# Hybrid decoder trunk on one core: half of the sample pages issued by GpSimd

## The chip, the cores and the metric

The kernel runs on one core of one Trainium2 chip. The metric is the device time of one execution in microseconds (us); lower is better. Three runs of the kernel before stand beside one profiled execution, from which the trace comes. All data are float32.

## The reference, cut to what matters

The program is one inference step of two layers for a prompt group of 512 tokens and a sample group of 8 sequences with 4 new tokens each. Layer 0 mixes tokens with native sparse attention, layer 1 with a gated delta rule; each is followed by a feed-forward block. The change touches only the sample part of layer 0. Each sample sequence has a past of 2048 tokens, held in 16 pages of 128 tokens that lie anywhere in a shared cache; a page table says where.

```
kc = compress_blocks(kv_full[:, :, 0], pe_k, w1_k, w2_k)      # pages, columns 0 and 1
vc = compress_blocks(kv_full[:, :, 1], pe_v, w1_v, w2_v)
p_cmp = masked_softmax(s, cvis) ...                           # attention over the compressed blocks
imp = jnp.einsum('bkgtn,nj->bktj', p_cmp, cmp_to_slc(nc, ns)) # importance of each 64-token block
top_s, top_i = lax.top_k(imp, ...)                            # 16 blocks are chosen
o_slc = attention over the chosen blocks of kv_full[:, :, 2:4] # pages, columns 2 and 3
o_win = attention over the last 512 tokens
o = g0 * o_cmp + g1 * o_slc + g2 * o_win
```

So of every page two halves are read: one "to compress" (128 KB) and one "to attend to" (128 KB).

## The kernel before

The program is written by hand: each engine has its own instruction stream, and semaphores tie the streams together. Names are `sp` (SyncE, issues nearly all loads), `pool` (GpSimd, issues the stores and adds a few squares), `pe` (TensorE), `act` (ScalarE) and `dve` (VectorE).

The sample part of layer 0 is a loop over the 8 sequences s = 0 to 7 on `pe`. In the pass of sequence s the stream of `pe` holds, in this order: `new_rows(s)`, `scores(s)` (L942 to L946), the first quarter of `compress(s + 1)` (L902, 16 matmuls in the trace), `importance(s)` (L950), the second quarter, `turn_window(s)` (L958), the third, `window_values(s)` (L967), the fourth, `values(s)` (L974 to L986) and `compressed(s + 1)` (L911, L914). So the next sequence is compressed inside the pass of the present one, and everything on `pe` that stands behind a quarter waits if that quarter waits. The last matmul of `compress(s)` adds one to the semaphore `w1_used`; the compression of the prompt has added one before, so `w1_used` is s + 1 once `compress(s)` is done. The last matmul of `values(s)` adds one to `so_done`.

Four buffers take pages: `page_cmp[0]`, `page_cmp[1]` for the halves to compress and `page_kv[0]`, `page_kv[1]` for the halves to attend to; sequence s uses the one of its parity. `wcache[s % 2]` takes the window rows of the cache, which `pool` then stores to the output `win_o` (L582), after which `win_stored` tells `sp` that the buffer is free.

Before it can issue a page, the issuing engine loads its number from the table in SBUF into a register. `places(s)` (L487) does this 16 times: a TENSOR_LOAD and two register instructions each. `pages(...)` (L492) issues the 16 loads of one buffer, with two register instructions ahead of each. In the kernel before both are done by `sp`, in `sequence(s)`: the 16 numbers, a wait, 16 pages to compress, a wait, 16 pages to attend to, and the window. The pages to compress of sequence s >= 3 wait for `w1_used` >= s - 1, that is for the end of `compress(s - 2)`, which used the same buffer.

Of the kernel before, what the change touches and what calls it, by code (L numbers as in the profile page):

```python
# [23 lines left out]
P = 128  # L24
D = 1024
KT = D // P
TP, NS, DT = 512, 8, 4
# [5 lines left out]
NPAGE, PAGE = 16, 128  # L33
PAST = NPAGE * PAGE
NPHYS = (NS * NPAGE * 5 + 3) // 4
# [87 lines left out]
def build(nc, x_in, mem_in, w_in, common_in, prompt_in, sample_in, gdn_in, pages_in, win_in, mcache_in, conv_in,  # L123
          state_in, table_in, y_out, kv_out, win_out, conv_out_p, conv_out_s, state_out_p, state_out_s, mem_out):
    with ExitStack() as ctx:
        sem = lambda name: ctx.enter_context(nc.semaphore(name))
# [27 lines left out]
        a = rest()  # L154
# [12 lines left out]
        a = free()  # L167
# [152 lines left out]
        in_prompt_t, in_sample_t, in_gdn_t = sem("in_prompt_t"), sem("in_sample_t"), sem("in_gdn_t")  # L320
        in_panel = [sem(f"in_panel{s}") for s in range(4)]
        in_cmp = [sem(f"in_cmp{s}") for s in range(2)]
        in_pages = [sem(f"in_pages{s}") for s in range(2)]
        in_mcache, in_mkv1, in_conv = sem("in_mcache"), sem("in_mkv1"), sem("in_conv")
        in_state = [sem(f"in_state{h}") for h in range(GH)]
# [132 lines left out]
        block = ctx.enter_context(nc.Block())  # L458


        @block.sync
        def _(sp):
            sp.dma_start(common_ap, common_in).then_inc(in_common, 16)
            sp.dma_start(memT, mem_in).then_inc(in_mem, 16)

            def panel(i):
                slot = i % 4
                if i >= 4:
                    f = free_at[i - 4]
                    if f == "w1":  # L470
                        sp.wait_ge(w1_used, NS)
                    elif f == "window":
                        sp.wait_ge(so_done, NS)
                        for b in range(2):
                            sp.wait_ge(win_stored[b], 16 * (NS // 2))
                    else:
                        sp.wait_ge(*f)
                sp.dma_start(ring[slot], w_in[src[i]]).then_inc(in_panel[slot], 16)

            panel(0)  # L480
            sp.dma_start(xT, x_in).then_inc(in_x, 16)
            for i in range(1, 4):
                panel(i)
            sp.dma_start(pages_sb[:, :], table_in).then_inc(in_table, 16)

            def places(s):
                return [sp.value_load(pages_sb[0:1, s * NPAGE + p:s * NPAGE + p + 1], min_val=0, max_val=NPHYS - 1)  # L487
                        for p in range(NPAGE)]

            def pages(s, at, to, cols, landed):  # L490
                for p in range(NPAGE):
                    sp.dma_start(to[s % 2][:, p, :],  # L492
                                 pages_in[bass.ds(at[p], 1), :, cols].rearrange("a p n -> (a p) n"))\
                        .then_inc(landed[s % 2], 16)

            def sequence(s):

                at = places(s)
                if s >= 3:
                    sp.wait_ge(w1_used, s - 1)  # L500
                pages(s, at, page_cmp, slice(0, 2 * P), in_cmp)
                if s == 1:
                    sp.wait_ge(prompt_done, 24)
                if s >= 2:
                    sp.wait_ge(so_done, s - 1)
                pages(s, at, page_kv, slice(2 * P, 4 * P), in_pages)
                if s >= 2:
                    sp.wait_ge(win_stored[s % 2], 16 * (s // 2))
                window(s)

            def window(s):
                sp.dma_start(wcache[s % 2], win_in[s]).then_inc(in_pages[s % 2], 16)

            for i in range(4, 14):
                panel(i)
                if i == 8:
                    sp.wait_ge(memn_ready, 2 * KT)
                    sp.wait_ge(mem_stored, 32)
                    sp.dma_start(mcache[0], mcache_in[0].rearrange("s p n -> p s n")).then_inc(in_mcache, 16)
                if i == 10:  # L520
                    sp.wait_ge(in_table, 16)
                    pages(0, places(0), page_cmp, slice(0, 2 * P), in_cmp)
            sp.wait_ge(prod_done, 7 * NSA_U)
            window(0)
            pages(0, places(0), page_kv, slice(2 * P, 4 * P), in_pages)
            sp.wait_ge(mix_mem, 5)
            sp.dma_start(prompt_ap, prompt_in).then_inc(in_prompt_t, 16)
            sp.wait_ge(w1_used, 1)
            sp.wait_ge(psum_ready, 2)
            sp.dma_start(sample_ap, sample_in).then_inc(in_sample_t, 16)  # L530
            for s in range(1, NS):
                sequence(s)
            for i in range(15, wbase["gdn_in"] + 14):
                if i == 15:
                    sp.wait_ge(smax_ready, NS)
                panel(i)
                if i == wbase["gdn_in"] + 3:
                    sp.wait_ge(prod_done, 7 * ubase["gdn_in"])
                    sp.wait_ge(*read_out(ubase["gdn_in"] - 1, "c21"))
                    sp.wait_ge(sq_used, KT + 2)  # L540
                    sp.dma_start(mkv[1], mem_out[1]).then_inc(in_mkv1, 16)
                    sp.dma_start(gdn_ap, gdn_in).then_inc(in_gdn_t, 16)
                    sp.dma_start(cbuf, conv_in).then_inc(in_conv, 16)
                    sp.dma_start(mcache[1], mcache_in[1].rearrange("s p n -> p s n")).then_inc(in_mcache, 16)
            for i in range(wbase["out1"], wbase["out1"] + 4):
                panel(i)
            for h in range(GH):
                if h == 0:
                    sp.wait_ge(conv_done, 20)
                    sp.wait_ge(mix_mem, 10)  # L550
                    sp.wait_ge(conv_stored, 32)
                if h == 1:
                    sp.wait_ge(prod_done, 7 * ubase["out1"])
                if h == 3:
                    sp.wait_ge(kq_done, 8)
                    sp.wait_ge(tr_ready, 8)
                sp.dma_start(sg[h], state_in[h].rearrange("p (a s) v -> p a s v", a=2)).then_inc(in_state[h], 16)
            for i in range(wbase["up1"], n_panels):
                panel(i)
            for k in range(KT):  # L560
                sp.wait_ge(h_ready, 2 * KT + k + 1)
                sp.dma_start(y_out[:, k, :], hT[:, k, :]).then_inc(y_stored, 16)
            sp.wait_ge(y_stored, 16 * KT)


        @block.gpsimd
        def _(pool):
            def add_squares(n):
                for k in range(1, KT - 1):
                    pool.wait_ge(sq_ready, n * KT + k + 1)  # L570
                    if k > 1:
                        pool.wait_ge(sq_added, 6 * (n - 1) + k - 1)
                    pool.tensor_tensor(sq_sum, sq_sum, sq[:, k % 2, :], ALU.add).then_inc(sq_added, 1)  # L573

            for l in range(2):
                pool.wait_ge(memkv_ready, 2 * l + 2)
                pool.dma_start(mem_out[l], (mkv0, mkv1_tmp)[l]).then_inc(mem_stored, 16)
            tiles_out(pool, "nsa_in", WV)
            pool.dma_start(kv_out, proj[:, CK:WV + 1, :]).then_inc(stored, 16)
            for s in range(NS):  # L580
                pool.wait_ge(in_pages[s % 2], 16 * (NPAGE + 1) * (s // 2 + 1))
                pool.dma_start(win_out[s], wcache[s % 2]).then_inc(win_stored[s % 2], 16)  # L582
            for n in (1, 2):
                add_squares(n)
            pool.wait_ge(conv_done, 20)
            pool.wait_ge(couts_ready, 1)
            pool.dma_start(conv_out_p, cout_p).then_inc(conv_stored, 16)
            pool.dma_start(conv_out_s, cout_s).then_inc(conv_stored, 16)
            pool.wait_ge(sup_done, 8)
            pool.dma_start(state_out_p, st_p).then_inc(stored, 16)  # L590
            for h in range(GH):
                pool.wait_ge(snew_ready, h + 1)
                pool.dma_start(state_out_s[h].rearrange("p (a s) v -> p a s v", a=2), sg[h]).then_inc(state_stored, 16)
            for n in (3, 4):
                add_squares(n)
            pool.wait_ge(stored, 32)
            pool.wait_ge(mem_stored, 32)
            pool.wait_ge(conv_stored, 32)
            for b in range(2):
                pool.wait_ge(win_stored[b], 16 * (NS // 2))  # L600
            pool.wait_ge(state_stored, 16 * GH)
# [288 lines left out]
        def pe_nsa_sample(pe):  # L890
# [2 lines left out]

            def compress(s, quarters):
                if 0 in quarters:
                    pe.wait_ge(in_cmp[s % 2], 16 * NPAGE * (s // 2 + 1))
                    pe.wait_ge(vnew_ready, s)
                    pe.wait_ge(kvc_ready, s)
                for quarter in quarters:
# [1871 lines left out]
```

## Time and profile before

| | us |
|---|---|
| median of three runs | 1996.64 (1996.47 to 1998.94) |
| profiled execution, its own time | 2001.48 |
| its span in the trace | 1999.7 |
| PE busy | 1893.6, 95% of the span |
| DVE busy | 1049.5, 52% |
| ACT busy | 520.3, 26% |
| POOL busy | 39.5, 2% |

The span is what the trace covers; the time of the execution is 1.8 us longer. The profiled execution is 4.8 us above the median. The sample part of layer 0 lies between about 355 and 550 us of the span. Register instructions, semaphores and DMA issues do not count as busy, so SyncE, which does nothing else, has no busy time at all, and the 2% of GpSimd leave its issues out; their times are read from the timeline.

### The profile page before, as it was taken

The numbers are of one execution on the slowest core, as the hardware profiler recorded it, in microseconds if no ns is written. First come the engines' busy times: TensorE is split into PE (matmuls) and PEld (weight loads), VectorE is DVE, ScalarE is ACT, GpSimd is POOL, SyncE is SP. The second block draws the span as 40 slices with busy tenths as digits, with TensorE's granted clock in tenths as the row PEclk, the third lists the DMA queues.
The fourth block names the chain that finished last, engine by engine and source line by source line (L and its number), as shares of the span: only waits on it lengthen the run. The fifth ranks groups of instructions, "written<-read, shape, count | busy, mean of one in ns | idle before, by whom it ended". The sixth has DMA issues, their size and how long they took to land.

```text
span 1999.7 us, 26775 instructions
## 1 busy us (share of the span) xinstructions
PE 1893.6 (95%) x10027; PEld 1522.5 (76%) x10027; DVE 1049.5 (52%) x2334; ACT 520.3 (26%) x1294; POOL 39.5 (2%) x48
## 2 busy tenths in 40 slices
PE   7999999998979999999989999899998999999997
PEld 6788555666758888888877787688876888888885
DVE  4441777655565444454446665456555544444444
ACT  2221777233312212100012523333341212210000
POOL 0000000000001000000010000000000000000001
PEclk9999999999989999999999999999998999999998
DMA  6532200566422222222233112100012122222211
GB/s 229 190 129 64 80 1 1 169 195 184 149 106 84 85 85 84 73 78 83 85 121 136 64 64 68 74 1 1 32 41 72 66 85 85 84 85 85 85 64 45
DMA packets 60801, 175.46 MB, mean 88 GB/s; under 512 B 6529, under 2 KB 39442, under 8 KB 47362
## 3 DMA queue, kind: packets, MB, share of 16 engines
q1 hardware_dynamic: 58050, 163.05, 24.4%
q0 software_dynamic: 2624, 10.70, 1.3%
q8 instruction: 81, 1.33, 0.3%
q14 instruction: 46, 0.38, 0.1%
HBM read 160.80 MB, written 12.93 MB: 87 GB/s over the span
## 4 chain that ended last, share of the span: by engine, by line
PE 82%; DVE 6%; SPq 5%; ACT 4%; issue 3%; DMA 1%; POOL 0%; DVEq 0%; POOLq 0%; ACTq 0%
PE psum L1818 58%; PE psum L1341 5%; SPq L492 3%; PE psum L758 2%; PE psum L902 2%; SPq L487 1%; PE psum L739 1%; ACT sbuf L802 1%; PE psum L721 1%; DVE sbuf L1677 1%; PE psum L1796 1%; PE psum L641 1%; PE psum L1899 1%; PE psum L1893 1%; PE psum L1931 1%
## 5 line engine op out<-in xcount | busy, mean ns | idle before, releaser
L1818 PE MATMUL psum<-sbuf 128*128 128x272 f32 x5152 | 1196.1, 393 | 4.5 <-ACT sbuf L2093 1.4
L1818 PEld LDWEIGHTS psum<-sbuf 128*128 128x128 f32 x5152 | 972.7, 190 | 215.6 <-issue 11.3
L1341 PE MATMUL psum<-sbuf 128*128 128x128 f32 (+3 forms) x1020 | 125.8, 279 | 12.4 <-DVE sbuf L1661 5.2
L1341 PEld LDWEIGHTS psum<-sbuf 128*128 128x128 f32 (+3 forms) x1020 | 118.7, 191 | 19.5 <-DVE sbuf L1661 6.0
L2043 ACT ACTIVATE sbuf<-sbuf 128x544 f32<-128x544 f32 x32 | 20.8, 651 | 396.9 <-DVE sbuf L2387 387.5
L902 PE MATMUL psum<-sbuf 128*128 128x256 f32 x448 | 106.7, 389 | 7.1 <-DMA sbuf<-in_pages 7.1
L2266 DVE TENSOR_TENSOR sbuf<-sbuf 128x512 f32<-128x512 f32 x92 | 63.4, 689 | 81.4 <-PE psum L1818 73.6
L902 PEld LDWEIGHTS psum<-sbuf 128*128 128x128 f32 x448 | 82.8, 190 | 24.0 <-DMA sbuf<-in_pages 8.1
L2270 DVE TENSOR_TENSOR sbuf<-sbuf 128x512 f32<-128x512 f32 x92 | 63.8, 693 | 52.2 <-PE psum L1818 50.5
L1520 ACT ACTIVATE sbuf<-psum 128x384 f32<-128x384 f32 (+2 forms) x84 | 40.2, 480 | 106.0 <-PE psum L1341 80.8
L2279 DVE TENSOR_TENSOR sbuf<-sbuf 128x512 f32<-128x512 f32 x92 | 63.1, 686 | 0.0
L2271 DVE TENSOR_TENSOR sbuf<-sbuf 128x512 f32<-128x512 f32 x92 | 63.1, 685 | 0.0
L2129 ACT ACTIVATE sbuf<-psum 128x272 f32<-128x272 f32 x32 | 12.8, 399 | 192.0 <-PE psum L1818 192.0
L2415 DVE SCALAR_TENSOR_TENSOR sbuf<-sbuf 128x1088 f32<-128x1088 f32 x32 | 41.4, 1293 | 36.7 <-ACT sbuf L2129 36.6
L802 ACT ACTIVATE sbuf<-sbuf 128x512 f32<-128x512 f32 (+3 forms) x96 | 52.4, 547 | 0.0
L758 PE MATMUL psum<-sbuf 128*64 128x128 f32 x480 | 41.4, 293 | 7.0 <-ACT sbuf L815 7.0
L851 DVE CUSTOM_DVE_ANT_0 sbuf<-psum,sbuf 128x512 f32<-128x512 f32 (+3 forms) x96 | 47.0, 548 | 0.2 <-issue 0.2
L2387 DVE TENSOR_TENSOR sbuf<-sbuf,psum 128x272 f32<-128x272 f32 x40 | 17.6, 439 | 55.8 <-PE psum L1818 55.8
L573 POOL TENSOR_TENSOR sbuf<-sbuf 128x544 f32<-128x544 f32 x24 | 27.9, 1164 | 949.9 <-ACT sbuf L2043 949.9
L2376 DVE TENSOR_TENSOR sbuf<-sbuf,psum 128x272 f32<-128x272 f32 x40 | 17.6, 439 | 52.9 <-PE psum L1818 52.9
L2374 DVE TENSOR_TENSOR sbuf<-sbuf,psum 128x272 f32<-128x272 f32 x40 | 17.5, 439 | 50.2 <-PE psum L1818 50.2
L739 PE MATMUL psum<-sbuf 128*128 128x128 f32 x240 | 38.7, 300 | 5.2 <-DVE sbuf L868 5.2
(390 smaller groups left out, 2026.9 us busy)
## 6 DMA issues: line engine op xcount, KB each, us to landing
sbuf<-in_w SPq DMA_DIRECT2D x100, 1024.0 KB, 4.9
sbuf<-in_pages SPq DMA_DIRECT2D x256, 128.0 KB, 2.4
sbuf<-in_mcache SPq DMA_DIRECT2D x2, 4096.0 KB, 15.4
sbuf<-in_win SPq DMA_DIRECT2D x8, 512.0 KB, 4.8
out_win_o<-sbuf POOLq DMA_DIRECT2D x8, 512.0 KB, 3.0
sbuf<-in_state SPq DMA_DIRECT2D x6, 512.0 KB, 5.7
out_state_s<-sbuf POOLq DMA_DIRECT2D x6, 512.0 KB, 3.1
sbuf<-in_x SPq DMA_DIRECT2D x1, 2176.0 KB, 11.9
```

Of the source, the lines that this page charges most:

```text
L492: sp.dma_start(to[s % 2][:, p, :], pages_in[bass.ds(at[p], 1), :, cols].rearrange("a p n -> (a p) n"))\
L739: last = pe.transpose(pt[:, P * r:P * (r + 1)], s_sb[n % 3][:, r, P * q:P * (q + 1)], ident)
L758: mm(o, vn[:, br, q, 64 * kv:64 * kv + 64], ptp[(groups(n) + q) % 3][:, 2 * br + kv, :], start=q == br == 0, stop=False)
L802: f(s_sb[n % 3][:, r, 0:nk], s_sb[n % 3][:, r, 0:nk], ACT.Exp, bias=st[:, r:r + 1], scale=-1.0, accum_out=st[:, 8 + r:9 + r])
L851: dve.tensor_tensor_reduce(s[:, r, 0:nk], bank(r)[:, 0:nk], PT["dist"][:, TP - nk:TP], slope(r % 2), -NEG, ALU.add, ALU.min, st[:, r:r + 1 ...
L902: last = mm(bank(6 + kind)[:, 2 * P * half:2 * P * (half + 1)], w1[kind][:, 8 * half + lp, :], page_cmp[s % 2][:, :, P * kind + 16 * lp:P ...
L1341: last = mm(bank(pair[x])[0:rows, width * (h - h0):width * (h - h0 + 1)], lhs(h), rhs(h), start=True, stop=True)
L1818: ins = mm(to, lhs(k), rhs(k), start=first and k == 0, stop=k == 3, skip_group_check=True)
L2266: tt(ws[0], w_[:, :, 0, P:2 * P], w_[:, :, 1, P:2 * P], ALU.add).then_inc(wsum_ready, 1)
L2270: tt(ws[1], ws[0], w_[:, :, 0, 0:P], ALU.subtract).then_inc(wsum_ready, 1)
L2271: tt(w_[:, :, 0, P:2 * P], w_[:, :, 0, 0:P], w_[:, :, 0, P:2 * P], ALU.subtract).then_inc(wsum_ready, 1)
L2279: tt(ws[2], w_[:, :, 1, 0:P], ws[1], ALU.subtract).then_inc(wsum_ready, 1)
```

## The change

`places` and `pages` take the engine as an argument. `sp` keeps the pages of sequence 0 and, for sequences 1 to 7, the pages to attend to (`to_attend`). The pages to compress of sequences 1 to 7 are issued by `pool` (`to_compress`), on two new semaphores `next_cmp`, and `pool` loads the page numbers for them itself. `to_compress(s)` stands in the stream of `pool` behind the store of the window of sequence s - 2, and waits for `w1_used` >= s. In `to_attend` the numbers are now loaded behind the wait for `so_done` (or `prompt_done`), where they stood ahead of all waits.

```diff
+        def places(eng, s):
+            return [eng.value_load(pages_sb[0:1, s * NPAGE + p:s * NPAGE + p + 1], min_val=0, max_val=NPHYS - 1)
+                    for p in range(NPAGE)]
+
+        def pages(eng, s, at, to, cols, landed):
+            for p in range(NPAGE):
+                eng.dma_start(to[s % 2][:, p, :],
+                              pages_in[bass.ds(at[p], 1), :, cols].rearrange("a p n -> (a p) n"))\
+                    .then_inc(landed[s % 2], 16)
...
-            def sequence(s):
-
-                at = places(s)
-                if s >= 3:
-                    sp.wait_ge(w1_used, s - 1)
-                pages(s, at, page_cmp, slice(0, 2 * P), in_cmp)
+            def to_attend(s):
                 if s == 1:
                     sp.wait_ge(prompt_done, 24)
                 if s >= 2:
                     sp.wait_ge(so_done, s - 1)
-                pages(s, at, page_kv, slice(2 * P, 4 * P), in_pages)
+                pages(sp, s, places(sp, s), page_kv, slice(2 * P, 4 * P), in_pages)
...
             for s in range(1, NS):
-                sequence(s)
+                to_attend(s)
...
+            def to_compress(s):
+                pool.wait_ge(w1_used, s)
+                pages(pool, s, places(pool, s), page_cmp, slice(0, 2 * P), next_cmp)
+
+            pool.wait_ge(in_table, 16)
+            pool.wait_ge(mix_mem, 5)
+            pool.wait_ge(psum_ready, 2)
+            to_compress(1)
             for s in range(NS):
                 pool.wait_ge(in_pages[s % 2], 16 * (NPAGE + 1) * (s // 2 + 1))
                 pool.dma_start(win_out[s], wcache[s % 2]).then_inc(win_stored[s % 2], 16)
+                if s + 2 < NS:
+                    to_compress(s + 2)
...
             def compress(s, quarters):
                 if 0 in quarters:
-                    pe.wait_ge(in_cmp[s % 2], 16 * NPAGE * (s // 2 + 1))
+                    if s:
+                        pe.wait_ge(next_cmp[s % 2], 16 * NPAGE * ((s + 1) // 2))
+                    else:
+                        pe.wait_ge(in_cmp[0], 16 * NPAGE)
```

On SyncE, sequence 2 stood like this before (page numbers, then 16 pages to compress, then behind `so_done` 16 pages to attend to; "ISA" is a register instruction):

```order
L487 TENSOR_LOAD page_table
L487 ISA x2
L492 ISA
L492 DMA sbuf<-in_pages 128x256
...
L492 ISA
L492 DMA sbuf<-in_pages 128x256
L492 ISA [waits so_done]
L492 DMA sbuf<-in_pages 128x256
```

and stands like this now, from the window of sequence 1 on:

```order
L509 DMA sbuf<-in_win 128x1024
L464 TENSOR_LOAD page_table [waits so_done]
L464 ISA x2
L464 TENSOR_LOAD page_table
...
L464 ISA x2
L469 ISA
L469 DMA sbuf<-in_pages 128x256
```

The wait for `so_done` moved ahead of the 16 page numbers, and the 16 pages to compress are gone.

On GpSimd the store of the window of sequence 0 was followed by that of sequence 1:

```order
L579 DMA out_kv<-sbuf 128x3264 [waits act_read,dve_read]
L582 DMA out_win_o<-sbuf 128x1024 [waits in_pages0]
L582 DMA out_win_o<-sbuf 128x1024 [waits in_pages1]
```

and now the 16 numbers and 16 pages of sequence 2 stand between them:

```order
L588 DMA out_win_o<-sbuf 128x1024 [waits in_pages0]
L464 TENSOR_LOAD page_table [waits w1_used]
L464 ISA x2
L464 TENSOR_LOAD page_table
...
L469 ISA
L469 DMA sbuf<-in_pages 128x256
L588 DMA out_win_o<-sbuf 128x1024 [waits in_pages1]
L464 TENSOR_LOAD page_table [waits w1_used]
```

The wait for `w1_used` stands ahead of the first of the 16 numbers, so none of the 32 steps behind it begins before it.

## Rows read from the trace of the kernel before

**Rows 1.** The page: span, and TensorE's granted clock in 40 slices, in tenths

```profile
span 1999.7 us, 26775 instructions
...
PEclk9999999999989999999999999999998999999998
```

**Rows 2.** What matrix work waited for, 353 to 550 us: total, times, longest

```profile
PE psum L902 <- DMA sbuf<-in_pages: 7.1, 4, 2.7
```

**Rows 3.** Timeline of PE (start, length, count, idle time before it)

```profile
359.37 3.75 PE L902 MATMUL psum<-sbuf 128*128 128x256 f32 x16
372.22 3.75 PE L902 MATMUL psum<-sbuf 128*128 128x256 f32 x16
382.20 1.94 PE L942 MATMUL psum<-sbuf 128*64 128x512 f32 x8
385.37 3.75 PE L902 MATMUL psum<-sbuf 128*128 128x256 f32 x16
...
496.97 5.42 PE L902 MATMUL psum<-sbuf 128*128 128x256 f32 x16 [2.68 <-DMA sbuf<-in_pages]
...
524.62 3.75 PE L902 MATMUL psum<-sbuf 128*128 128x256 f32 x16
```

**Rows 4.** Timeline of SyncE's issues (start, length of the group)

```profile
373.53 18.29 SPq L492 DMA_DIRECT2D sbuf<-in_pages  x32
391.87 0.43 SPq L512 DMA_DIRECT2D sbuf<-in_win  x1
```

**Rows 5.** The chain that ended last, 353 to 420 us (start, length)

```profile
354.39 0.30 DVE sbuf L874
354.84 0.33 SPq L492
355.36 0.33 SPq L492
...
364.07 0.28 SPq L487
...
373.53 0.34 SPq L492
```

**Rows 6.** Busy time of each engine in two stretches

```profile
core 0: us, PE busy (x) PEld busy (x) DVE busy (x) ACT busy (x) POOL busy (x), PEclk, DMA share, GB/s
359.37:375.97 16.60, 16.60 (x82) 12.89 (x81) 14.21 (x44) 3.04 (x8) 0.53 (x1) 1.00 0.52 165
375.97:385.37 9.40, 8.65 (x76) 5.69 (x76) 1.12 (x3) 6.88 (x17) 0.00 (x0) 1.00 0.75 213
```

**Rows 7.** Timeline of GpSimd: two issues of its own, back to back

```profile
1232.07 0.58 POOL L587 DMA_DIRECT2D out_conv_p<-sbuf  x1 [191.71 <-ACT sbuf L2078]
1232.65 0.54 POOL L588 DMA_DIRECT2D out_conv_s<-sbuf  x1
```

**Rows 8.** DMA issues of the page: KB each, us from issue to landing

```profile
sbuf<-in_pages SPq DMA_DIRECT2D x256, 128.0 KB, 2.4
sbuf<-in_win SPq DMA_DIRECT2D x8, 512.0 KB, 4.8
out_win_o<-sbuf POOLq DMA_DIRECT2D x8, 512.0 KB, 3.0
```

**Rows 9.** Granted clock (third from the end) behind the 2.68 us wait

```profile
499.00:501.00 2.00, 2.00 (x6) 1.53 (x6) 1.40 (x5) 0.00 (x0) 0.00 (x0) 0.50 0.93 255
501.00:505.00 4.00, 4.00 (x18) 3.10 (x17) 2.00 (x8) 0.00 (x0) 0.00 (x0) 0.95 0.79 227
```

**Rows 10.** Register loads and page issues of SyncE: shortest, median, longest in ns

```profile
L487 SPq TENSOR_LOAD <-page_table x144: 260/267/1339, 87.2 to 512.0; - x144
L492 SPq DMA_DIRECT2D sbuf<-in_pages x256: 332/333/1520, 96.4 to 529.0; - x128
```

**Rows 11.** Timeline of VectorE between scores and importance of one sequence

```profile
415.57 0.48 DVE L1139 TENSOR_SCALAR sbuf<-sbuf 64x516 f32<-64x516 f32 x1
417.20 0.35 DVE L1096 TENSOR_SCALAR sbuf<-sbuf 64x24 f32<-64x24 f32 x2
```

More of the change, by code:

```diff
@@ L322, in build @@
         in_cmp = [sem(f"in_cmp{s}") for s in range(2)]
+        next_cmp = [sem(f"next_cmp{s}") for s in range(2)]
         in_pages = [sem(f"in_pages{s}") for s in range(2)]
@@ L484, in _ @@
             sp.dma_start(pages_sb[:, :], table_in).then_inc(in_table, 16)
[L486 to L494, printed above, removed]
-            def sequence(s):
-                at = places(s)
-                if s >= 3:
-                    sp.wait_ge(w1_used, s - 1)
-                pages(s, at, page_cmp, slice(0, 2 * P), in_cmp)
+            def to_attend(s):
                 if s == 1:
@@ L521, in _ @@
                     sp.wait_ge(in_table, 16)
-                    pages(0, places(0), page_cmp, slice(0, 2 * P), in_cmp)
+                    pages(sp, 0, places(sp, 0), page_cmp, slice(0, 2 * P), in_cmp)
             sp.wait_ge(prod_done, 7 * NSA_U)
             window(0)
-            pages(0, places(0), page_kv, slice(2 * P, 4 * P), in_pages)
+            pages(sp, 0, places(sp, 0), page_kv, slice(2 * P, 4 * P), in_pages)
             sp.wait_ge(mix_mem, 5)
```

## The prediction

> **What bounds the kernel now.** I read the page first: TensorE is busy nearly everywhere and its granted clock stays at eight tenths or more in every slice, at nine in all but three [rows 1], so whatever lengthens TensorE's stream lengthens the kernel. Next the waits of the sample part: what TensorE loses there to page loads is 7.1 us, in four waits ahead of L902, the longest 2.7 [rows 2]. Then the timelines, to see who is late. On TensorE the first quarter of `compress` starts at 359.37 (sequence 1), 385.37 (sequence 2), and at last at 524.62 (sequence 7) [rows 3]: six intervals in 165.25 us, 27.5 each. On SyncE the issues leave no room: 32 pages take 18.29 us, the window follows at 391.87 [rows 4], and 16 page numbers take from 364.07 to 373.53, 9.46 us [rows 5]. Together 9.5 + 18.3 + 0.4 = 28.2 us for a sequence. So SyncE's issuing, not the transfers, paces the loop, by about one us over what TensorE needs.
>
> The reader should also see two lengths on TensorE. `compress` runs from 359.37 to 375.97 (its fourth quarter starts at 372.22 and takes 3.75), 16.6 us with the small steps between the quarters; from its end to the start of the next there are 9.4 us [rows 3, 6].
>
> **What the change takes away.** SyncE drops 16 pages of 32 per sequence. Its loop falls to 9.5 for the numbers, half of 18.3 for the pages and 0.4, about 19 us, and is no longer the pace. If nothing else came in, the 7.1 us of waits would go, and with them the slow matmuls behind the last: that quarter took 5.42 us and not 3.75, 1.67 us more [rows 3], with the granted clock at 0.50 (1.2 GHz and not 2.4) in the stretch 499 to 501 [rows 9]. That is 8.8 us at most.
>
> **What it adds: a chain in place of a prefetch.** Before, the pages of s waited for the end of `compress(s - 2)`. Now all 32 steps of `to_compress(s)` stand behind `w1_used` >= s, which is the end of `compress(s - 1)`. The two buffers no longer overlap. From that moment TensorE has 9.4 us until it wants the pages [rows 6], and GpSimd must do this in them:
>
> - 16 page numbers. GpSimd loads none before the change. The nearest row is SyncE's, 9.46 us from the first load to the first issue behind the last [rows 5]; I take it as it is. Bounds: no GpSimd row shows less; from above, SyncE's longest load is 1.34 us against 0.27 at the median [rows 10], which for all 16 would be 17 us more.
> - 16 page issues. SyncE starts one every 0.52 us, of which 0.33 is the issue itself [rows 5], so 0.19 us goes to the register steps around it. GpSimd's own issues, the only two back to back, start 0.58 us apart [rows 7]. I take 0.58 + 0.19 = 0.77 us; 15 steps make 11.5 us. Bounds: SyncE's 0.52 (7.8 us), and SyncE's longest issue of 1.52 us [rows 10], which gives 1.71 a step (25.7 us). Between them I keep to the row of the engine that will do it.
> - the landing of the last page: 2.4 us, SyncE's median for the same transfer [rows 8]; GpSimd's own stores of four times the size land in 3.0.
> - the semaphore hop: 0.15 us, from the end of the VectorE step at 354.69 to SyncE's issue at 354.84 [rows 5].
>
> Together 23.5 us, where 9.4 are free: TensorE stands still for 14.1 us ahead of every `compress` from 2 to 7. What is queued behind it is the whole remainder of the pass: `importance`, the choice of blocks on VectorE, the values. Nothing there can run ahead, so the interval from one `compress` to the next becomes 16.6 + 23.5 = 40.1 us. `compress(1)` is spared; its pages are issued during the prompt's part.
>
> Behind such a wait the clock will have fallen. The row at hand costs 1.67 us after a wait of 2.68 [rows 3]; I take 1.67 for each, 41.8 us an interval. Zero and twice that are the bounds.
>
> Six intervals of 41.8 are 250.8 us; before they were 165.25. **The sum is +85.5 us.** On the span 1999.7 that is 2085.2, with the 1.8 us around it 2087.0, and less the 4.8 us by which the profiled execution stands above the median, 2082.
>
> **What I cost at nothing.** SyncE now loads its numbers behind the wait. For sequence 1 that puts them on a path: released at 354.69, plus 0.15, 9.5 for the numbers, 9.1 for the pages, 0.4 and 4.8 for the window [rows 4, 5, 8], the data are there at about 378.6; `scores(1)` wants them at 382.20 [rows 3], 3.6 us later. For later sequences the release is the end of the values two sequences back, more than 40 us ahead, for 23 us of work. The cover is the length of the pass; with a pass of 27 us it would still hold by some 4. GpSimd's window store for s now stands behind the 32 steps for s + 1; SyncE needs that buffer again for s + 2, a pass later. The squares that GpSimd adds come only after the loop. The bytes are the same, and the 16 DMA engines are about half busy to three quarters in these stretches [rows 6], so bandwidth decides nothing.
>
> **A rule beside the rows.** In the stretch in which GpSimd will issue, VectorE runs single-input instructions between scores and importance, such as L1139 (0.48 us) and L1096 (two in 0.35) [rows 11]. If a GpSimd issue can't proceed while one of them runs, these 0.8 us and a few short ones like them, say 1.5 us a pass, come on top: 9 us in all.
> The Trainium skill says this of DMAs issued from GpSimd (SBUF — State Buffer, section "SBUF: two separate sides"): their descriptors are written by GpSimd's own cores, which are locked out while VectorE runs a copy or scalar instruction in its two-port mode. Its figures, 620 ns alone and 3100 ns beside such a copy, would by an estimate from that page add up to 2.5 us wherever an issue meets one; no row of this trace shows a GpSimd issue stretched that way.
>
> **The rivals.**
> 1. *GpSimd is slower at these steps than SyncE and its own rows say.* It has never loaded a register here, and two issues in a row are little evidence. With 0.1 to 0.3 us more for each of the 31 steps, 3 to 9 us an interval, the time is 2101 to 2138; chance 0.21. With more than that it is above 2138; chance 0.10.
> 2. *VectorE holds up the issues*, as above: 2091, chance 0.08.
> 3. *GpSimd keeps SyncE's pace and the clock costs nothing*: 9.46 + 7.8 + 2.4 + 0.15 = 19.8, an interval of 36.4, 218.4 in all, +53: 2050. Chance 0.07.
> 4. *The other side: the chain is hidden.* It decides at the point where the interval is what it was: 27.5 - 16.6 = 10.9 us from the end of one `compress` to the last page of the next. Below 9.4 us the waits vanish, -8.8 us: 1988. That would need GpSimd to load numbers and issue pages side by side, or 0.2 us and not 0.5 for each step. SyncE's rows speak against it, and the numbers of a buffer all stand ahead of its issues. Chance 0.03.
> 5. *The two cancel*, 10.9 us give or take half a us: chance 0.01.
>
> **How the numbers follow.** The forecast, a chain of 21 to 26 us with the clock's share (2065 to 2100), has 0.50; its middle is 2082. The range 2050 to 2138 takes in rivals 1 (its first half), 2 and 3. Left out are the far part of rival 1, and rivals 4 and 5: 0.14, and some of rival 3. Below 0.2% (4 us), no measurement here tells a change from none. Faster 0.03, same 0.01, slower 0.96.
>
> **What would show it.** In the profile of the changed kernel: the wait of `compress` (now L913) for pages grows from 7.1 us in four to about 85 in six, each near 14, at `compress(2)` to `compress(7)`; the quarter of sequence 2 starts near 399.5 and not 385.37; GpSimd's timeline holds seven groups of 16 issues, about 0.77 us a step, each 9.5 us behind the end of a `compress`; each first quarter behind a wait takes about 5.4 us with a granted clock of 0.50; SyncE's 16 pages to attend to land well before `scores`. I am wrong if GpSimd's groups start before the end of the previous `compress`, if the issues are spaced by more than 1 us or the numbers take over 12, or if TensorE's wait is for the pages to attend to.

## The result and the profile after

The changed kernel takes 2098.70 us (median of four runs, 2095.21 to 2100.27) against 1996.86 before (four runs): ratio 1.0506, 95% interval 1.0494 to 1.0519. It is slower, by about 101 us; the forecast was 2082 with a range of 2050 to 2138.

The page of the changed kernel; the columns are those of [rows 1]:

```profile
span 2098.6 us, 27115 instructions
PE 1909.1 (91%) x10027; PEld 1532.7 (73%) x10027; DVE 1049.3 (50%) x2334; ACT 519.4 (25%) x1294; POOL 100.8 (5%) x160
PEclk9999999888778999999999999999998999999999
```

The same 10,027 matmuls fill 91% of the span and not 95%. The granted clock is below nine tenths in six slices in a row, two of them at seven tenths, where the sample part lies; before, it was in one of these. GpSimd's busy time grew from 39.5 to 100.8 us. Unlike what "Time and profile before" says, the page does count GpSimd's issues as busy: the 112 new ones, of 0.55 us each, are the 61 us. What matrix work waited for there, 353 to 660 us (total, times, longest), to be held against [rows 2]:

```profile
PE psum L913 <- DMA sbuf<-in_pages: 91.4, 6, 16.9
```

Six waits, one ahead of each `compress` from 2 to 7. The timeline of PE around the first two, to be held against [rows 3]:

```profile
362.27 3.75 PE L913 MATMUL psum<-sbuf 128*128 128x256 f32 x16
...
375.12 3.75 PE L913 MATMUL psum<-sbuf 128*128 128x256 f32 x16
...
403.19 6.29 PE L913 MATMUL psum<-sbuf 128*128 128x256 f32 x16 [14.85 <-DMA sbuf<-in_pages]
...
418.58 3.75 PE L913 MATMUL psum<-sbuf 128*128 128x256 f32 x16
...
446.44 5.17 PE L913 MATMUL psum<-sbuf 128*128 128x256 f32 x16 [14.66 <-DMA sbuf<-in_pages]
...
622.34 5.94 PE L913 MATMUL psum<-sbuf 128*128 128x256 f32 x16 [16.91 <-DMA sbuf<-in_pages]
```

Six intervals lie between 362.27 and 622.34: 260.1 us where there were 165.25, so 94.8 of the 98.9 us between the two spans. The other 4.1 are a start of the first `compress` that is 2.9 us later (362.27 and not 359.37; executions of one kernel differ by about that much, as shown below), and 1.2 us behind the last start, where the slow quarter after the last wait alone costs 2.2.

`compress(2)` ends at 422.33 (418.58 + 3.75). The chain that ended last, from there to the next `compress` (start, length):

```profile
422.37 0.30 POOLq L464
422.70 0.16 POOLq L464
422.94 0.29 POOLq L464
...
430.86 0.15 POOLq L464
431.09 0.04 POOLq L469
431.19 0.49 issue
431.68 0.04 POOLq L469
431.72 0.06 POOL sbuf L469
431.78 0.49 issue
```

and its end, from the last of the 16 issues:

```profile
439.95 0.51 issue
440.46 5.93 DMA sbuf<-in_pages
446.40 0.04 issue
446.44 3.64 PE psum L913 x9
```

This is the predicted chain: numbers, issues, landing, all behind the end of the previous `compress`. GpSimd's timeline has the group of issues and the window's store behind it:

```profile
431.70 9.32 POOL L469 DMA_DIRECT2D sbuf<-in_pages  x16 [33.28 <-issue]
441.00 0.54 POOL L588 DMA_DIRECT2D out_win_o<-sbuf  x1
```

and SyncE's has the pages to attend to at the same time:

```profile
435.94 9.43 SPq L469 DMA_DIRECT2D sbuf<-in_pages  x16
445.41 0.45 SPq L509 DMA_DIRECT2D sbuf<-in_win  x1
```

Term by term for this interval: numbers 422.33 to 431.70, 9.4 us (9.6 were forecast with the hop); 15 steps of 0.585 us from the first issue to the last, 8.8 us (11.5 forecast); from the last issue to the start of the matmuls at 446.44, 6.0 us (2.4 forecast). Together 24.1 us, where the forecast had 23.5. Over all six it is 148.1 us against 141: five between 24.0 and 24.8, the last 26.4.

### The profile page after: what moved, and what is told of

The parts are those of the page before. It is cut to its first block, busy times and chain, and to the rows that moved or that the text cites. A ratio compares the mean times of both kernels' runs of the same rounds, so it can differ in the third digit from the quotient of the medians.

```text
span 2098.6 us, 27115 instructions
## 1 busy us (share of the span) xinstructions
PE 1909.1 (91%) x10027; PEld 1532.7 (73%) x10027; DVE 1049.3 (50%) x2334; ACT 519.4 (25%) x1294; POOL 100.8 (5%) x160
## 4 chain that ended last, share of the span: by engine, by line
PE 83%; DVE 5%; issue 5%; ACT 3%; POOLq 2%; DMA 2%; POOL 0%; DVEq 0%; SPq 0%
PE psum L1829 55%; PE psum L913 6%; PE psum L1352 5%; POOLq L464 2%; DMA sbuf<-in_pages 2%; PE psum L766 2%; PE psum L747 1%; PE psum L729 1%; PE psum L1807 1%; ACT sbuf L810 1%; DVE sbuf L1688 1%; PE psum L649 1%; PE psum L1910 1%; PE psum L1904 1%; PE psum L1942 1%
## 5 line engine op out<-in xcount | busy, mean ns | idle before, releaser
L913 PE MATMUL psum<-sbuf 128*128 128x256 f32 x448 | 119.6, 424 | 91.4 <-DMA sbuf<-in_pages 91.4
L1352 PE MATMUL psum<-sbuf 128*128 128x128 f32 (+3 forms) x1020 | 125.0, 278 | 12.4 <-DVE sbuf L1672 5.2
L469 POOL DMA_DIRECT2D sbuf<-in_pages x112 | 61.4, 549 | 431.6 <-issue 428.0
L2398 DVE TENSOR_TENSOR sbuf<-sbuf,psum 128x272 f32<-128x272 f32 x40 | 17.5, 438 | 55.8 <-PE psum L1829 55.8
L2387 DVE TENSOR_TENSOR sbuf<-sbuf,psum 128x272 f32<-128x272 f32 x40 | 17.5, 438 | 52.9 <-PE psum L1829 52.9
```

Of the source, the lines that this page charges most:

```text
L469: eng.dma_start(to[s % 2][:, p, :], pages_in[bass.ds(at[p], 1), :, cols].rearrange("a p n -> (a p) n"))\
L913: last = mm(bank(6 + kind)[:, 2 * P * half:2 * P * (half + 1)], w1[kind][:, 8 * half + lp, :], page_cmp[s % 2][:, :, P * kind + 16 * lp:P ...
L1352: last = mm(bank(pair[x])[0:rows, width * (h - h0):width * (h - h0 + 1)], lhs(h), rhs(h), start=True, stop=True)
```

## The experiments

Each experiment was measured beside runs of the kernel before, and its ratio is to those. The theory: the loss comes from where the wait stands (behind `compress(s - 1)`), and the engine matters little. The rival: GpSimd is the worse issuer, wherever it waits. The gap between the terms needed a second question: why does the last page take 6 us to land?

**The early wait.** GpSimd does all it does in the changed kernel, but waits for the last user of its own buffer.

```diff
             def to_compress(s):
-                pool.wait_ge(w1_used, s)
+                if s == 1:
+                    pool.wait_ge(w1_used, 1)
+                elif s == 2:
+                    pool.wait_ge(first_done, 2)
+                else:
+                    pool.wait_ge(w1_used, s - 1)
```

> The changed kernel with one condition changed: to_compress(s) waits for the last use of its own buffer (w1_used >= s - 1, for s = 2 first_done >= 2), as before the change, and no longer for the compression of s - 1. GpSimd still loads the numbers and issues the pages. Theory (the late wait is the loss, 24.3 us of steps against 9.4 us of cover): the six waits of TensorE for pages vanish, and with them the slow matmuls, so it comes out at or below the kernel before, about 1988 us. Rival (GpSimd is too slow or too crowded an issuer whatever it waits for): the waits shrink but stay, and the time is 2010 or more.

Measured: 1993.45 us (ten runs) against 1997.56, ratio 0.9979 (0.9970 to 0.9989). The timeline of PE:

```profile
359.23 3.75 PE L918 MATMUL psum<-sbuf 128*128 128x256 f32 x16
...
385.22 3.75 PE L918 MATMUL psum<-sbuf 128*128 128x256 f32 x16
...
402.55 1.09 PE L990 MATMUL psum<-sbuf 128*128 128x128 f32 x8 [0.72 <-DVE sbuf L1192]
...
411.53 3.75 PE L918 MATMUL psum<-sbuf 128*128 128x256 f32 x16
...
516.68 3.75 PE L918 MATMUL psum<-sbuf 128*128 128x256 f32 x16
```

No `compress` waits any more; 359.23 to 516.68 is 157.5 us for six intervals, 7.8 less than in the profile of the kernel before. The short waits that are left are for VectorE (L1192 above all) and ScalarE. GpSimd still takes its time: in this kernel too its 16 pages go out in 9.3 us behind 9.4 of numbers, and a page of its own lands after 4.8 us at the median, now under the cover of a whole pass. One changed condition is worth about 105 us, and the rival falls. The time is 5 us above the 1988 expected: 4 us were gained and not 9.

**The late wait alone, on SyncE.** The kernel before, with nothing moved to GpSimd.

```diff
+                if s >= 2:
+                    sp.wait_ge(w1_used, s)
                 at = places(s)
-                if s >= 3:
-                    sp.wait_ge(w1_used, s - 1)
```

> The kernel before, all pages issued by SyncE, with the late wait alone: for s >= 2 the wait for w1_used >= s stands ahead of the 16 numbers. Theory: the same chain on SyncE, 0.15 + 9.46 + 7.8 + 2.4 us, and about 2.4 us for the clock, an interval of 38.8 us and not 27.5, +68: about 2065 us. The remainder to 2099 is then what the landing beside the other group of pages costs (6.0 us and not 2.4) and GpSimd's step of 0.58 for 0.52. Rival (the engine is the loss): no wait of note, 1997 us.

Measured: 2069.59 us against 1997.56, ratio 1.0352 (1.0336 to 1.0368). Six waits, 64.2 us:

```profile
396.45 5.37 PE L902 MATMUL psum<-sbuf 128*128 128x256 f32 x16 [10.10 <-DMA sbuf<-in_pages]
...
435.13 6.49 PE L902 MATMUL psum<-sbuf 128*128 128x256 f32 x16 [11.02 <-DMA sbuf<-in_pages]
```

So 70 of the 101 us are had without GpSimd (72 by the medians). The landing was 2.4 us at the median here, and 2.7 for the last page ahead of the first wait; SyncE issues the second 16 pages behind the first 16, so the two groups are not issued at the same time.

**The pages to attend to later.** The changed kernel; only SyncE is held back, so that its pages do not run beside GpSimd's. It also loads its 16 numbers ahead of its waits, so that the pages go out at once when the wait ends.

```diff
+                at = places(sp, s)
                 if s == 1:
                     sp.wait_ge(prompt_done, 24)
                 if s >= 2:
                     sp.wait_ge(so_done, s - 1)
-                pages(sp, s, places(sp, s), page_kv, slice(2 * P, 4 * P), in_pages)
+                    sp.wait_ge(next_cmp[s % 2], 16 * NPAGE * ((s + 1) // 2))
+                pages(sp, s, at, page_kv, slice(2 * P, 4 * P), in_pages)
```

> The changed kernel, in which SyncE begins the pages to attend to of sequence s only when the pages to compress of s have landed, with its numbers loaded ahead of the waits. Nothing is changed on GpSimd. Theory (the last page lands 6.0 us after its issue because both groups and the window's store share the DMA engines): it lands in about 2.4 us, 3.6 us less in six intervals, -22: about 2077 us. Rival (6 us is what a page issued by GpSimd takes): 2099.

Measured: 2077.49 us against 1997.56, ratio 1.0401 (1.0385 to 1.0416). The DMA issues, first of the changed kernel and then of this one (KB each, median us to landing):

```profile
sbuf<-in_pages POOLq DMA_DIRECT2D x112, 128.0 KB, 3.8
out_win_o<-sbuf POOLq DMA_DIRECT2D x8, 512.0 KB, 7.1
```

```profile
sbuf<-in_pages POOLq DMA_DIRECT2D x112, 128.0 KB, 2.4
out_win_o<-sbuf POOLq DMA_DIRECT2D x8, 512.0 KB, 3.3
```

A page from GpSimd lands in 2.4 us, like one from SyncE, when SyncE's pages do not run beside it. The last page of each group, for which TensorE waits, took 5.6 to 6.3 us in the six passes of the changed kernel and 2.4 to 2.8 here. Holding work back made the kernel 21 us faster. The busy share of the DMA engines (next to last) and GB/s, first of the changed kernel over the end of a landing, then of this one:

```profile
436.00:441.00 5.00, 0.00 (x0) 0.00 (x0) 1.89 (x6) 0.00 (x0) 4.70 (x9) 0.50 0.84 269
441.00:446.40 5.40, 0.00 (x0) 0.00 (x0) 0.00 (x0) 0.00 (x0) 0.55 (x2) 0.50 0.98 313
```

```profile
391.00:395.20 4.20, 0.03 (x1) 0.03 (x1) 0.00 (x0) 0.00 (x0) 2.48 (x5) 0.50 0.74 251
```

The engines are full, at 0.98, while TensorE waits for the last of GpSimd's pages; in the experiment they are not. The Trainium skill says that DMAs from several engines run on the same 16 DMA engines and interleave, so that issuing from more of them saves only the time of issuing (DMA: Bandwidth & Descriptors, section "Issuing engines are not separate DMA queues"). These rows agree that the engines are shared: with both queues at work their share is 0.98. They also show a price, the later landing.

**The numbers first.** The changed kernel, with GpSimd's 16 register loads ahead of its late wait.

```diff
             def to_compress(s):
+                at = places(pool, s)
                 pool.wait_ge(w1_used, s)
-                pages(pool, s, places(pool, s), page_cmp, slice(0, 2 * P), next_cmp)
+                pages(pool, s, at, page_cmp, slice(0, 2 * P), next_cmp)
```

> The changed kernel with the 16 page numbers loaded by GpSimd ahead of the wait for w1_used >= s. Theory: 9.4 us leave the chain in each of six intervals, -56: about 2042 us, with waits of about 5.5 us in place of 15. Rival (the issue or the landing would be late anyway, because the other group of pages fills the DMA engines at that time): less than half of it, above 2070.

Measured: 2019.96 us against 1997.56, ratio 1.0108 (1.0093 to 1.0124): 79 us less than the changed kernel, where 56 were expected and the rival had less than half of that. A row each of GpSimd, PE and SyncE shows why it is more:

```profile
375.69 6.98 POOL L469 DMA_DIRECT2D sbuf<-in_pages  x12 [168.32 <-PE psum L914]
```

```profile
387.19 5.42 PE L914 MATMUL psum<-sbuf 128*128 128x256 f32 x16 [2.68 <-DMA sbuf<-in_pages]
```

```profile
389.27 8.21 SPq L469 DMA_DIRECT2D sbuf<-in_pages  x16
```

The pages now land by 387.2, before SyncE starts on its own at 389.27. So the 9.4 us of numbers went, and the collision with them: the 56 us of the numbers and the 21 of the experiment before add up to 77, near the 79 measured. I had held the two for separate. The waits left are 2.5 to 5.1 us where about 5.5 were expected.

**The wait filled with matmuls.** The changed kernel; ahead of `compress(s)`, s >= 2, TensorE runs matmuls that nobody reads, into the bank that `compress` overwrites.

```diff
+                    for _ in range(56 if s > 1 else 0):
+                        mm(bank(6)[:, 0:2 * P], w1[0][:, 0, :], w1[1][:, 0:2, :], start=True, stop=True)
                     pe.wait_ge(next_cmp[s % 2], 16 * NPAGE * ((s + 1) // 2))
```

> The changed kernel in which TensorE fills the wait for pages: ahead of compress(s), s = 2 to 7, it runs 56 matmuls of the same shape on weights already there, into a bank that compress then overwrites (13 us of 15). Theory (the half-rate stretch behind each wait is the clock that fell while TensorE stood still, 14.6 us in six first quarters, and 2.2 in the last): every first quarter takes 3.75 us at full clock and the time falls by 12 to 15 us, to about 2085. Rival (the slow first quarter comes from something else, such as the operands still being written): no change, 2099, or above it by what the added matmuls overrun.

Measured: 2138.07 us against 1998.22, ratio 1.0700 (1.0683 to 1.0716). A miss in the size of the filling: each of these is two matmuls in the trace, so 56 took 24.4 us and overran the wait. The quarters behind were at full clock, but the time says nothing. With 32:

> As the kernel that fills the wait, with 32 added matmuls in the program and not 56: the trace shows two for each, 0.218 us apart, so 56 took 24.4 us and overran the wait by 9, while 32 take 14.0 us of a wait of 14.6 to 16.9. Theory (the slow first quarter is the fallen clock): first quarters of 3.7 us at full clock, 14.6 us less in six of them: about 2084. Rival (clock and length of the quarter have nothing to do with the idle time): 2099.

Measured: 2084.66 us against 1996.99, ratio 1.0437 (1.0420 to 1.0454), so 0.69% or 14 us less than the changed kernel. The first, second and last filled waits:

```profile
386.77 14.08 PE L907 MATMUL psum<-sbuf 128*128 128x256 f32 x64
402.58 3.75 PE L912 MATMUL psum<-sbuf 128*128 128x256 f32 x16 [1.73 <-DMA sbuf<-in_pages]
...
428.56 14.08 PE L907 MATMUL psum<-sbuf 128*128 128x256 f32 x64
443.47 3.75 PE L912 MATMUL psum<-sbuf 128*128 128x256 f32 x16 [0.83 <-DMA sbuf<-in_pages]
...
592.52 14.08 PE L907 MATMUL psum<-sbuf 128*128 128x256 f32 x64
609.52 6.63 PE L912 MATMUL psum<-sbuf 128*128 128x256 f32 x16 [2.92 <-DMA sbuf<-in_pages]
```

Five of six quarters are back at 3.75 us with the same late pages (the last of a group lands after 5.7 to 6.7 us here). Only the one behind a rest of 2.92 us is still slow. The granted clock is third from the end, first in the changed kernel (idle until 403.19, then the slow quarter):

```profile
400.00:403.00 3.00, 0.00 (x0) 0.00 (x0) 0.00 (x0) 0.00 (x0) 0.00 (x0) 0.50 0.96 347
403.00:405.00 2.00, 1.81 (x4) 1.51 (x5) 0.00 (x0) 0.00 (x0) 0.00 (x0) 0.50 1.05 385
407.00:409.00 2.00, 2.00 (x7) 1.60 (x7) 0.00 (x0) 0.00 (x0) 0.00 (x0) 0.65 0.30 119
```

and then in this one, with the wait filled:

```profile
403.00:405.00 2.00, 2.00 (x11) 1.72 (x10) 0.00 (x0) 0.00 (x0) 0.00 (x0) 1.00 0.96 282
```

The slow quarters are the clock's, at 0.50 (1.2 GHz and not 2.4), and TensorE's own idleness lowers it.

**Both early.** The kernel with the early wait, and on GpSimd the numbers ahead of that wait, the pages ahead of the window's store.

```diff
+            to_compress(2)
             for s in range(NS):
+                if 3 <= s + 2 < NS:
+                    to_compress(s + 2)
                 pool.wait_ge(in_pages[s % 2], 16 * (NPAGE + 1) * (s // 2 + 1))
                 pool.dma_start(win_out[s], wcache[s % 2]).then_inc(win_stored[s % 2], 16)
-                if s + 2 < NS:
-                    to_compress(s + 2)
```

> The kernel with the early wait, and on GpSimd also the numbers ahead of that wait and the pages ahead of the window's store. If the early wait alone already brings every page in time, so that the loop is held by VectorE and TensorE themselves, nothing more is to be had: the same as the early wait alone, 1988 to 1994 us. Rival (pages that land just in time still cost something now and then): 2 to 4 us less.

Measured: 1991.55 us (six runs) against 1998.22, ratio 0.9969 (0.9956 to 0.9981). The early wait alone, once more:

> The kernel with the early wait once more, on the chip of the other two: a gain of 0.1 to 0.4% over the kernel before, if the 8.8 us of waits and slow matmuls are what the issuing engine had cost; a ratio at 1.000 if the first measurement was chance.

Measured: 1992.70 us (ten runs), ratio 0.9973 (0.9964 to 0.9983). Both beat the kernel before by 0.2 to 0.3%, in two sets of runs; between the two no difference can be told. The early wait alone is the version to keep: SyncE's queue is relieved, and the wait stays where it was before the change.

## Why the prediction was right, and where it was not

**The mechanism** was right and is shown: the changed condition takes the prefetch away. With the condition put back the kernel is below the kernel before; with the condition alone, on SyncE, 70 of 101 us are there.

By experiments, in the ratios above: the late wait on SyncE +70 us; GpSimd in its place, with SyncE's pages held back, +10 more (1.0401 against 1.0352); the two groups of pages beside each other +21. That makes 101. By the medians the three are 72, 8 and 22.

**The numbers on GpSimd**: taken over from SyncE at 9.46 us and 0.15 for the hop, measured 9.4 to 9.7 with the hop. A load takes 283 ns at the median on GpSimd and 267 on SyncE.

**The issue step** was mis-sized: 0.77 us, measured 0.585. I added SyncE's 0.19 us of register steps to GpSimd's own 0.58. In the changed kernel an issue of GpSimd takes 0.546 us and the next starts 0.04 us behind its end, so the register instructions between two issues add 0.04 and not 0.19. That the 0.58 of [rows 7] is as long as a whole step is chance: there one issue took 0.58 by itself. The term was 2.8 us too much in the interval above. Over all six it was 13.4 too much, since GpSimd also stopped for 0.34 us in two of the groups and for 2.13 in the last, as the last section shows.

**The landing** was the step that failed: 2.4 us, measured 5.6 to 6.3. It rests on the sentence that "bandwidth decides nothing". The bytes were the same, but they were no longer in a row: before, one queue issued both groups one behind the other; now two do at the same time, and the DMA engines' share stands at 0.98 just when TensorE waits. The 0.52 and 0.75 that I had read [rows 6] were not the whole picture even before: behind the late pages at 499 it was 0.93 [rows 9]. The window's store, issued right behind GpSimd's group, is not the cause by itself: it stood there in the experiment too, where the last page landed in 2.4 to 2.8. The term was 3.5 us an interval too little, 21 in all, and the experiment with SyncE held back gave 21. That these two errors nearly cancelled is luck: the chain came out at 24.1 for 23.5 in the interval above, and 7.1 us over the forecast in all six.

**The clock**: 1.67 us for each first quarter, measured 2.54, 1.42, 2.56, 2.94, 2.94 and 2.19, mean 2.4, inside the bounds: 14.6 us for 10.0. Five of them lie inside the six intervals, 12.4 us. The row I took came behind a rest of 2.68 us, and here the rests are 15. But the rest's length does not set the price: behind one of 14.66 us the quarter lost 1.42, less than the 1.67 behind 2.68, and behind those of 10 to 11 us with the late wait on SyncE it lost 1.6 to 3.0. What sets it among these is open.

**From 2082 to 2098.7**: 9.3 us are the intervals, 260.1 and not 250.8 (the chain 7.1, the clock 2.4, less 0.2 of rounding). 4.1 lie outside them, where I had put nothing. 3.2 come from the profile: I took off 4.8 us, by which the profiled execution of the kernel before stood above the median, and that of the changed kernel stands 1.6 above.

**What was costed at nothing**: the numbers behind `prompt_done`, the window's store behind 32 other steps, and the squares cost nothing; there is no wait for the pages to attend to, in the changed kernel or with the early wait. The gain of 8.8 us that SyncE's relief was to bring at most, which I had as rival 4's price, shows as 7.8 us of the intervals between two profiles, one of which stood 4.8 us above its median. By the medians it is 4 to 7 us, in the kernels with the early wait and with both early.

**Rival 1** (slower steps) did not come about, nor did **rival 2**. GpSimd's 112 page issues take 546 ns at the shortest and at the median, 771 at the longest, with VectorE's single-input instructions in between; in the group from 431.70 on, this one fell into the middle and the 16 issues still took 9.32 us:

```profile
435.69 0.48 DVE L1150 TENSOR_SCALAR sbuf<-sbuf 64x516 f32<-64x516 f32 x1
```

What the Trainium skill says of VectorE locking out GpSimd's descriptor writing (SBUF — State Buffer, section "SBUF: two separate sides") is thus not seen in these issues at the sizes of its figures; whether any of these instructions ran in the mode that it means, no run here shows.

**Left open**: the first `compress` began at 357.5 to 362.3 us in the executions profiled, with the changes and without. In the changed kernel's own the scores ahead of it ran at half clock (3.40 us for L953, 1.95 before). The kernel with the early wait, profiled twice, began at 359.23 with these scores at full clock (1.94 us) and at 361.88 with them at half (3.63), so it differs between executions of one kernel. Why, no run shows. The 8 to 10 us that GpSimd itself costs were not tested one by one. From the end of one `compress` to the start of the next the traces give 127.1 us in six intervals with SyncE held back and 120.9 with the late wait on SyncE. The 6.2 us between them are about what GpSimd's longer step (15 times 0.07 us, six times) and its stop in the last group come to, 8 us.

## What to carry to other kernels

When loads move to another queue, read first behind what they now wait: a buffer's load must wait for the last user of that buffer, not for the newest user of its neighbour, and the length of the issuing chain (here about 19 us for 16 dynamic pages) is only free as long as a whole pass covers it. Then ask which other transfers the move puts beside them: unchanged bytes in two queues can still finish later than in one. Register loads that feed dynamic addresses belong ahead of the wait.

## What the runs showed of the hardware that was not expected

GpSimd issues dynamic loads not much slower than SyncE: 0.585 us a step against 0.515 to 0.52, and its pages land in 2.4 us at the median when SyncE's pages do not run beside them.

In the last group, for sequence 7, GpSimd stops for 2.13 us behind the eleventh issue, in the changed kernel and in the one with the early wait alike, though they are 110 us apart at that point. The row of the changed kernel:

```profile
614.16 2.90 POOL L469 DMA_DIRECT2D sbuf<-in_pages  x5 [2.13 <-issue]
```

and that of the kernel with the early wait:

```profile
504.75 3.01 POOL L469 DMA_DIRECT2D sbuf<-in_pages  x5 [2.13 <-issue]
```

In the kernel with both early one window store fewer stands ahead of this group, and there the stop comes one issue later, behind the twelfth:

```profile
489.79 2.31 POOL L469 DMA_DIRECT2D sbuf<-in_pages  x4 [2.10 <-issue]
```

So it goes with the place in GpSimd's instruction stream and not with the time; what GpSimd waits for there no row names. It is why the last of the six intervals is 2 us longer than the others.

Holding back SyncE's transfers made the kernel 21 us faster, and idle TensorE filled with matmuls that nobody needs made it 14 us faster: both only repair what the late wait had broken.
